# First attention tile: the reciprocal of the softmax denominators as a logarithm and a negative exponential on ScalarE

## The reference, cut to what matters

```python
def _attend(q, k, v):
    # q: (B, Q, Hkv, G, hd); k, v: (B, K, Hkv, hd) -> (B, Q, Hkv, G, hd)
    s = jnp.einsum('bqkgd,bskd->bkgqs', q, k).astype(jnp.float32) * ATTN_SCALE
    p = jax.nn.softmax(s, axis=-1).astype(v.dtype)
    return jnp.einsum('bkgqs,bskd->bqkgd', p, v)
```

## Time and profile before

| | |
|---|---|
| runs | 1882.88, 1901.16, 2072.66 us; median 1901.16 |
| profiled execution: its time | 1883.87 us |
| profiled execution: span of the slowest core (core 5) | 1882.3 us |
| spans of the cores | 1874.8 to 1882.3 us |
| busy | TensorE 93%, VectorE 58%, ScalarE 37%, GpSimd 29% |
| TensorE clock, mean of the core | 0.984 of 2.4 GHz |

### The profile page before, as it was taken

The page is one execution under the profiler, slowest core; times in us unless marked ns, Lnnn a source line. Parts: engine busy times, 40 slices in busy tenths (PEclk is TensorE's granted clock), DMA queues, the critical chain, the costliest instruction groups (busy, mean ns, idle before and its releaser), DMA issues.

```text
span 1882.3 us, 28154 instructions; the slowest of 8 cores (1874.8 to 1882.3 us)
## 1 busy us (share of the span) xinstructions
PE 1750.0 (93%) x8708; PEld 811.0 (43%) x8708; DVE 1089.3 (58%) x1409; ACT 693.8 (37%) x1186; POOL 539.0 (29%) x563
## 2 busy tenths in 40 slices
PE   2779999999999989788899999999999999999999
PEld 1334545545453444332344444444333444444443
DVE  1445446444445677697888788788554544544444
ACT  2540111111124555475766666666544211111110
POOL 4220001000014376365555455455253100000000
PEclk9889999999999999998999999999999999999999
DMA  9914245051512211110535435435484213203013
GB/s 179 238 48 82 38 86 102 16 95 25 94 19 56 57 73 51 52 34 1 119 67 90 98 62 101 93 56 94 68 139 80 46 23 59 40 4 68 0 51 129
DMA packets 39905, 133.28 MB, mean 71 GB/s; under 512 B 4304, under 2 KB 4560, under 8 KB 39120
## 3 DMA queue, kind: packets, MB, share of 16 engines
q0 software_dynamic: 30400, 106.97, 31.6%
q1 hardware_dynamic: 9360, 24.51, 3.8%
HBM read 211.16 MB, written 15.73 MB: 121 GB/s over the span
## 4 chain that ended last, share of the span: by engine, by line
PE 81%; DVE 6%; issue 4%; ACT 3%; DMA 3%; POOL 2%; DVEq 0%; ACTq 0%; POOLq 0%
PE ps L628 17%; PE ps L600 16%; PE ps L595 16%; PE ps L1202 12%; PE ps L1288 5%; PE ps L1305 4%; PE ps L839 3%; DMA arena<-w_ffn_in 2%; DVE tmpf L1327 1%; DVE tmpf L1311 1%; PE ps L1325 1%; PE ps L933 1%; PE ps L1301 1%; PE ps L1302 1%; DVE tmpf L532 1%
## 5 line engine op out<-in xcount | busy, mean ns | idle before, releaser
L632 DVE SCALAR_TENSOR_TENSOR xT<-ps,cols,xT 128x512 f32<-128x512 f32 x384 | 285.4, 750 | 269.7 <-PE ps L628 261.3
L612 ACT ACTIVATE tmpf<-ps 128x512 f32<-128x512 f32 (+1 forms) x198 | 113.2, 572 | 739.2 <-PE ps L595 697.0
L1202 PE MATMUL ps<-arena,ring 128*128 128x512 bf16 x1024 | 286.8, 381 | 13.6 <-ACT tmpf L1226 5.5
L614 DVE TENSOR_TENSOR arena<-ps,tmpf 128x512 bf16<-128x512 f32 (+1 forms) x198 | 131.1, 662 | 253.4 <-PE ps L600 190.3
L628 PE MATMUL ps<-arena,ring 128*128 128x512 bf16 (+1 forms) x928 | 238.6, 372 | 11.0 <-DVE xT L632 5.6
L600 PE MATMUL ps<-arena,ring 128*128 128x512 bf16 (+1 forms) x1088 | 245.1, 368 | 0.0
L595 PE MATMUL ps<-arena,ring 128*128 128x512 bf16 (+1 forms) x976 | 218.6, 367 | 0.0
L628 PE MATMUL ps<-arena 128*128 128x512 bf16 (+1 forms) x656 | 173.7, 368 | 0.7 <-DVE xT L632 0.7
L1351 ACT ACTIVATE tbf<-ps 128x512 bf16<-128x512 f32 x256 | 147.0, 599 | 63.4 <-PE ps L1288 44.1
L1202 PEld LDWEIGHTS ps<-arena,ring 128*128 128x128 bf16 x1024 | 99.1, 98 | 144.7 <-issue 32.8
L600 PEld LDWEIGHTS ps<-arena,ring 128*128 128x128 bf16 x1088 | 106.9, 98 | 116.1 <-issue 2.8
(11 more groups left out here) (155 smaller groups left out, 2244.4 us busy)
## 6 DMA issues: line engine op xcount, KB each, us to landing
ring<-w_in POOLq DMA_DIRECT2D x40, 512.0 KB, 6.6
ring<-w_ffn_in POOLq DMA_DIRECT2D x29, 512.0 KB, 8.1
ring<-w_ada POOLq DMA_DIRECT2D x27, 512.0 KB, 14.6
xT<-x POOLq DMA_DIRECT2D x8, 1024.0 KB, 52.6
ring<-w_ab POOLq DMA_DIRECT2D x16, 512.0 KB, 5.3
ring<-w_o POOLq DMA_DIRECT2D x16, 512.0 KB, 6.0
out<-xT SPq DMA_DIRECT2D x32, 256.0 KB, 2.5
arena<-w_ffn_in POOLq DMA_DIRECT2D x15, 512.0 KB, 8.3
```

The source lines that it names most:

```text
L612: P.op("act", lambda e: e.activation(out=tmpf[:, sg, 0:n], in_=ps[pg][:, 0:n], func=AF.Silu), reads=[ps_b[pg]], writes=[tmpf_b[sg]])
L614: P.op("dve", lambda e: e.tensor_tensor(out=act[pa][:, jj, 0:n], in0=ps[pu][:, 0:n], in1=tmpf[:, sg, 0:n], op=ALU.mult), reads=[ps_b[pu], ...
L632: P.op("dve", lambda e: e.scalar_tensor_tensor(out=b["xsl"](m), in0=ps[po][:, 0:n], scalar=cols[:, b["ig"], m:m + 1], in1=b["xsl"](m), op0 ...
L1202: ins = e.matmul(ps[bank][:, 0:512], w3[:, k, c0:c0 + 128], rhs(k), start=(k == 0), stop=(k == nk - 1))
```

## The change

For the eight heads of tile 0 alone, the reciprocal on VectorE is left out. In its place ScalarE takes the logarithm of bank 5 one step after `den`, and the exponential of its negative one step later, both into `rec`; the multiplication on VectorE (`scale_out`) follows that. Heads of tiles 1 to 3 keep the reciprocal.

```diff
                 def den():
                     P.op("pe", lambda e: e.matmul(ps[5][:, 0:512], ones_f[:], acc, start=False, stop=True),
                          reads=[acc_b, onesf_b], writes=[ps_b[5]])
-                    P.op("dve", lambda e: e.reciprocal(out=rec, in_=ps[5][:, 0:512]), reads=[ps_b[5]], writes=[rec_b])
+                    if i > 0:
+                        P.op("dve", lambda e: e.reciprocal(out=rec, in_=ps[5][:, 0:512]), reads=[ps_b[5]], writes=[rec_b])
+                        scale_out()
+
+                def scale_out():
                     P.op("dve", lambda e: e.tensor_tensor(out=Q[:, h, :], in0=ps[po][:, 0:512], in1=rec, op=ALU.mult),
                          reads=[ps_b[po], rec_b], writes=[Q_b[h]])
+
+                def ln():
+                    P.op("act", lambda e: e.activation(out=rec, in_=ps[5][:, 0:512], func=AF.Ln), reads=[ps_b[5]], writes=[rec_b])
+
+                def inv():
+                    P.op("act", lambda e: e.activation(out=rec, in_=rec, func=AF.Exp, scale=-1.0), reads=[rec_b], writes=[rec_b])
+                    scale_out()
                 defer[g + 3] = join
                 defer[g + 7] = den
+                if i == 0:
+                    defer[g + 8] = ln
+                    defer[g + 9] = inv
```

## The result

The changed kernel takes 1874.78 us in the median of 16 runs, the kernel before 1882.85 in 16 runs beside it. The ratio, from the executions in which no die ran slower than the other, is 0.9935 (95% interval 0.9911 to 0.9958): by the ratio 12 us less (the interval is 8 to 17), where the prediction had 14.6. The two medians are only 8.1 us apart, and the stretches counted further down come to 8.3, which speaks for the low end of the interval. The profiled execution took 1873.19 us, the span of its slowest core (core 7) is 1871.6.

What follows compares the result with a forecast made beforehand. VectorE was taken to bound tile 0. Against 1883.87 us: -22.0 (reciprocals and clock) + 4.9 (Ln/Exp pair) + 2.5 (last head) = -14.6, so 1869 us; range 1856 to 1889, the forecast's own 1861 to 1877.

Steps and rivals of the forecast that it cites:

- Tile 1 passes on what tile 0 saves: Tile 1: TensorE is busy 132.5 of 135 us, so an earlier start ends the kernel earlier.
- The waits in S3 and S5 and the clock behind them: Two tile 0 stretches between den products: TensorE's 2.65 and 3.85 us Fourier waits shrink; clock recovery gives 5.1 us.
- On the chain it is 5 x 3.37 = 16.9 us.: Tile 0: five of seven reciprocals lie on the chain of waits, each counted at full length.
- its low end of 11.6: Tile 0: lower bound in us for the reciprocals' removal, if another chain of additions and buffers is close behind.
- S4: Tile 0 stretch between den products, 14.2 us: its reciprocal is off the chain, counted as no gain; pair costs 0.7.
- Its sign that something is wrong: Tile 0: the prediction is wrong if the stretches between den products stay at 14 us and above.
- The pair at 0.7 us per head, 4.9 in all: Tile 0, seven heads: added Ln and Exp on ScalarE cost 4.9 us, bounds nothing to 2.2 us per head.
- The last head at 2.5 us: Tile 1, steps 7 and 8: head 7's Ln and Exp bring two table loads, costing 2.5 us (1.0 to 4.0).
- Tables otherwise, loads for tile 1, the multiplication: No table loads in heads 0 to 6, hidden-state loads stay hidden, multiplication moved two steps: counted 0.
- the close second chain: Rival, tile 0: another chain close behind; removal gives 11.6 us, net gain 4 to 5, 1879 us; chance 0.25.
- ScalarE blocked: Rival, steps 8 to 10 of each head: Ln blocks ScalarE's queue, 8 us slower, 1892 us; chance 0.05.
- alternating tables: Rival: two table loads in every head, 25.7 us over seven heads, 6 us slower, 1890 us; chance 0.03.

Runs made afterwards that it cites:

- e1: Changed kernel without Ln and Exp in tile 0: reciprocals left out, nothing in their place, outputs not scaled by denominators; ratio 0.9920 to the kernel before.
- e5: Changed kernel with the Ln/Exp pair only for heads 2 and 4 of tile 0, the others keeping the reciprocal; ratio 0.9955 to the kernel before.
- e6: Changed kernel with the Ln/Exp pair only for heads 0, 1, 3, 5 and 6 of tile 0; ratio 0.9970 to the kernel before.
- c3: Kernel before, with head 4's reciprocal and multiplication in tile 0 issued two steps later, behind the Fourier evacuation; ratio 0.9990 to the kernel before.
- e7: Changed kernel with head 7's reciprocal kept and GpSimd's additions of tile 0 left out (work missing); ratio 0.9878 to the kernel before.
- c2: Changed kernel, head 7's reciprocal kept, Ln/Exp one step later, TensorE adding each tile 0 head's last six steps, not three; 1865.96 us, ratio 0.9908.

## Why the prediction was right, and where its sizes were off

The forecast was 14.6 us, the measurement is 12 by the ratio and 8.1 by the medians; the range held it. The mechanism was right where it was forecast to be largest, in S3 and S5. The closeness of the sum owes something to luck: e1 puts the removal at 13.6 us in tile 0 instead of 22.0, the pair took back 2.0 instead of 4.9 and the last head 3.3 instead of 2.5, so the two largest errors, 8.4 and 2.9 us, partly cancel. By its steps:

*Tile 1 passes on what tile 0 saves.* Right: tiles 1 to 3 take 411.6 to 412.0 us with every kernel that leaves the last head alone.

*The waits in S3 and S5 and the clock behind them.* Right, and the larger part of the gain. Forecast, net of the pair: 3.4 + 1.7 - 0.7 = 4.4 us in S3 and 3.4 + 3.4 - 0.7 = 6.1 in S5; measured on the slowest core 4.0 and 5.4, as the mean of the cores 2.6 and 4.8. For S3 the forecast was made from a core with the full wait and the low clock; only four cores have the wait of 2.65 us, and only two of these the clock of 0.91. e5 and e6 tie the waits to heads 2 and 4, and c3 shows for head 4 that the place in the queue is the cause. For head 2 this wasn't tried.

*"On the chain it is 5 x 3.37 = 16.9 us."* This is the term that was too large: with the clock it was 22.0, and e1's 13.6 lies much nearer to its low end of 11.6. In S2, S6 and S7 it stood for 3.4 us each, 2.7 net; measured are 1.4, 1.9 and 0.7 us, 4 instead of 8. A reciprocal on the chain was taken at its whole length, as if nothing came soon behind it. e7 and c2 show how soon something comes: with VectorE busy for 9.3 and 7.3 us in S2 and 8.2 and 7.9 in S6, S2 ends at 12.3 and 12.0 us and S6 at 11.5 in both. The 12.0 is what the sum had for S2; its 10.8 for S6 no run reaches. In e7 TensorE and ScalarE are each busy for 10.4 to 11.0 us of these stretches; that the float32 product, the exponentials and the matmuls in turn make up the rest is argued from that and from the chain in S6, not shown. S1, where the chain showed no reciprocal and the sum had +0.7, gained 1.7, which made up for some of it.

*S4.* Forecast +0.7, measured +1.4. On the mean of the cores it is 1.7, as the clock falls on two. GpSimd is last there (e7), and was so before. The prediction named a buffer chain of both engines and didn't look at which stretch had GpSimd's Fourier additions in it, nor at what the reciprocal's leaving would do to them. That S4 shrinks when GpSimd's work does is shown (e7), and that it grows with the loss of head 3's reciprocal (e5, e6). Its sign that something is wrong, stretches that stay at 14 us and above, came true in S1, S3 and S4 (15.3, 14.8 and 15.6 us).

*The pair at 0.7 us per head, 4.9 in all.* Measured 2.0 in tile 0, by e1. As the mean of the cores that is 0.5 in S2 and 1.1 in S5 and S7 and nothing in S6; S4, longer in e1, hides 0.8. The prediction's upper bound of 2.2 us per head was far off. TensorE and ScalarE hand over to each other with or without the pair, which may be why.

*The last head at 2.5 us.* Measured 3.3. Two loads of 1.28 us each and no more: Ln starts 1.30 us after the load's start. The drain of 1.38 us per switch that the Trainium skill has ("ScalarE: Activation LUTs", What ACT_TABLE_LOAD costs) shows here no more than before: the load at 915.35 us starts as the ACTIVATE ahead of it ends.

*Tables otherwise, loads for tile 1, the multiplication.* No load in heads 0 to 6; SyncE issued the loads of the hidden states at 886.8 us, and their first use was at 905.0, without a wait.

Of the rivals, the close second chain came nearest in its reason and had the gain at 4 to 5 us. The truth lies between it and the forecast: tile 0 was forecast at -17.1 us and measured at -11.6 as the mean of the cores and -12.6 on the slowest. With the 3.3 us of the last head that is a gain of 8.3 us, to which the rival's 4 to 5 are nearer than the forecast's 14.6; to the ratio's 12 the forecast is nearer. ScalarE blocked and alternating tables didn't occur.

## What to carry to other kernels

A long instruction on an engine with time to spare can still be worth its length, or more, if it stands in an in-order queue in front of something that TensorE waits for: look at what is queued behind it before counting busy time, and try moving it by a step or two first (c3 got most of S5's gain for nothing). The length of a piece on the chain isn't what its removal gives: pieces of 3.37 us gave 0.7 to 1.9 us in S2, S6 and S7 and 5.4 in S5, the pair's cost taken off, and S1, whose reciprocal wasn't on the chain, gained 1.7. The sum lay near its low end, which came from a stretch in which the piece was off the chain. Read a stretch on all cores before building a term on it: S3 had 4.0 us to give on one core and 1.8 to 3.9 on the others. When work moves to ScalarE, leave out the instances that fall among functions of another table: seven heads paid 2 us together, the eighth 3.3 alone.

## What the runs showed of the hardware

The granted clock fell from the 2.4 GHz level to the 1.2 GHz one behind single stops of TensorE of 2.65, 3.85 and 3.1 us, in S3, S5 and (e1) S4. It didn't always: a stop of 2.65 us in S3 of the kernel before lowered it on two of the four cores that had it, one of 2.00 us in S4 of the changed kernel on two of eight, that of 3.1 us in e1 on six of eight; the 3.85 us in S5 lowered it on every core. The pairs of cores price the low clock: S3 took 18.7 us with it and 17.1 without behind the same stop, S4 17.0 and 15.6. That is 1.6 and 1.4 us on top of the stop. So the same program on the same chip has stretches of two lengths, and one core isn't enough to compare two kernels in them.

An addition on VectorE with two operands in SBUF took 0.69 us where GpSimd did nothing (core 5 before, 883 to 889 us), 1.13 on average over tile 0 of the changed kernel, with GpSimd's additions beside many, and 0.83 with most of GpSimd's gone (e7). GpSimd's Fourier additions in S4 took 1.31 us beside a reciprocal on VectorE and 1.54 without it. The Trainium skill ("SBUF — State Buffer", SBUF: two separate sides) has the two engines take one shared pair of ports by turns. The trace agrees as far as the additions go. In VectorE's time the result hardly depends on it, since that had become slack; in S4, where GpSimd is last, it may.
